# Where seven modulation tiles of the second layer are computed: four among the q, k and v groups, three in the attention steps, and the second q tile's weights awaited by pieces

## What is computed

```python
mod = (s_lat @ ada_w[layer] + ada_b[layer])[:, None, :]     # s_lat = silu(c); mod_c the same with silu(c_ctx)
sh1, sc1, g1, sh2, sc2, g2 = jnp.split(mod, N_MOD, axis=-1) # six parts of 1024
h = modulate(x, norm1_g[layer], sh1, sc1)                   # rms_norm(x, g) * (1 + scale) + shift
h_c = modulate(ctx, norm1_g[layer], csh1, csc1)
q, k, v = qkv_heads(h, odd_w_qkv[i], odd_q_g[i], odd_k_g[i])  # q and k: rms_norm per head of 64
q_c, k_c, v_c = qkv_heads(h_c, odd_w_qkv[i], odd_q_g[i], odd_k_g[i])
y = _merge(neighbourhood_attention(q, k, v, k_c, v_c, odd_rpb[i])) @ odd_w_o[i]
x = x + g1 * y
x = x + g2 * conv_ffn(modulate(x, norm2_g[layer], sh2, sc2), ...)
```

## Time and profile before

| | |
|---|---|
| median of 3 runs | 2199.19 us (2197.61 to 2202.82) |
| the profiled execution, its own time | 2198.84 us |
| its span, of which the rows speak | 2197.2 us |
| TensorE busy | 2080.6 us, 95% of the span |
| VectorE, ScalarE, GpSimd busy | 845.2, 585.0, 71.5 us |
| TensorE's granted clock, mean | 0.984 of full speed |

### The profile page before, as it was taken

One profiled execution on the slowest core, in us unless ns is written; L12 is line 12 of the kernel. 1 busy time (PEld: TensorE's weight loads), 2 busy tenths in 40 slices (PEclk: granted clock), 3 DMA queues, 4 the chain that ended last, 5 costly groups with the idle time before them and its releaser, 6 DMA issues.

```text
span 2197.2 us, 27385 instructions
## 1 busy us (share of the span) xinstructions
PE 2080.6 (95%) x11614; PEld 1389.7 (63%) x11614; DVE 845.2 (38%) x1566; ACT 585.0 (27%) x1002; POOL 71.5 (3%) x119
## 2 busy tenths in 40 slices
PE   7999999999999899999998999999999989999997
PEld 5787887878777479999888833433434333434332
DVE  4355533453583767745465521211111111111012
ACT  4223322342332656534365210000000000000001
POOL 0000000000000320000040000000000000000000
PEclk9999999999999999999999999999999999999998
DMA  9543433422421664545524899999999999999996
GB/s 368 200 152 115 153 115 128 155 79 100 171 77 56 222 219 154 180 159 184 191 97 186 325 370 403 428 428 428 427 428 427 428 428 427 427 427 428 427 409 268
DMA packets 164819, 592.88 MB, mean 270 GB/s; under 512 B 9138, under 2 KB 83890, under 8 KB 139348
## 3 DMA queue, kind: packets, MB, share of 16 engines
q1 hardware_dynamic: 163028, 589.68, 68.0%
q10 hardware_dynamic: 1664, 1.39, 0.2%
HBM read 590.00 MB, written 1.05 MB: 269 GB/s over the span
## 4 chain that ended last, share of the span: by engine, by line
PE 78%; DMA 14%; DVE 3%; ACT 2%; issue 2%; SPq 1%; ACTq 0%; DVEq 0%
PE ps L1007 23%; PE ps L290 14%; PE ps L292 14%; PE ps L291 14%; DMA ring<-in_w_up_dram 10%; DMA ring<-in_ada_w_dram 3%; PE ps L956 3%; PE ps L975 2%; PE ps L436 2%; DVE wr L1141 2%; ACT big L2126 1%; PE ps L1032 1%; PE ps L655 1%; PE ps L444 0%; SPq L2268 0%
## 5 line engine op out<-in xcount | busy, mean ns | idle before, releaser
L1007 PE MATMUL ps<-ring,big 128*64 128x512 f32 x3008 | 684.9, 607 | 56.2 <-DMA ring<-in_w_up_dram 35.6
L1007 PEld LDWEIGHTS ps<-ring,big 128*64 128x64 f32 x3008 | 245.2, 140 | 465.7 <-issue 456.8
L290 PE MATMUL ps<-h_hi,wr 128*128 128x512 f32 (+1 forms) x960 | 337.1, 351 | 2.3 <-DVE big L1378 1.1
L1141 DVE TENSOR_TENSOR wr<-ring,wr 128x1024 fp32r<-128x1024 f32 (+1 forms) x248 | 286.5, 1211 | 134.6 <-ACT wr L1826 134.5
L291 PE MATMUL ps<-h_lo,wr 128*128 128x512 f32 (+1 forms) x960 | 330.4, 344 | 0.0
L292 PE MATMUL ps<-h_hi,wr 128*128 128x512 f32 (+1 forms) x960 | 330.2, 344 | 0.0
L1826 ACT CAST wr<-ring 128x1024 fp32r<-128x1024 f32 (+1 forms) x248 | 239.3, 1032 | 115.9 <-PE ps L292 93.3
L290 PEld LDWEIGHTS ps<-h_hi,wr 128*128 128x128 f32 x960 | 182.5, 190 | 37.1 <-issue 10.4
L291 PEld LDWEIGHTS ps<-h_lo,wr 128*128 128x128 f32 x960 | 182.6, 190 | 22.0 <-issue 1.4
L292 PEld LDWEIGHTS ps<-h_hi,wr 128*128 128x128 f32 x960 | 182.4, 190 | 21.6
L2126 ACT ACTIVATE big<-ps,s 128x128 f32<-128x128 f32 x64 | 24.0, 456 | 357.7 <-PE ps L956 357.7
(11 more groups left out here) (343 smaller groups left out, 2620.8 us busy)
## 6 DMA issues: line engine op xcount, KB each, us to landing
ring<-in_w_gate_dram SPq DMA_DIRECT2D x62, 2048.0 KB, 22.1
ring<-in_w_up_dram SPq DMA_DIRECT2D x59, 2048.0 KB, 18.3
ring<-in_w_down_dram SPq DMA_DIRECT2D x57, 2048.0 KB, 22.0
ring<-in_ada_w_dram SPq DMA_DIRECT2D x24, 2048.0 KB, 11.4
ring<-in_ffn_w_up_dram SPq DMA_DIRECT2D x44, 1024.0 KB, 7.6
ring<-in_ffn_w_down_dram SPq DMA_DIRECT2D x16, 1408.0 KB, 6.2
ring<-in_w_in_dram SPq DMA_DIRECT2D x9, 2048.0 KB, 7.9
ring<-in_odd_w_qkv_dram SPq DMA_DIRECT2D x6, 2048.0 KB, 7.8
```

What stands on the lines that cost most here:

```text
L290: e.matmul(o, l[0], r[0], start=first, stop=False)
L1007: ins = e.matmul(pts[hf][HALF[z], :], lhs[:, k, HALF[z]], wt, start=k == 0, stop=False, skip_group_check=True)
L1141: e.tensor_tensor(wr[:, x], ring[:, x], h.bitcast(F32), SUB).then_inc(s_wlo, 1)
```

## The change

Tiles 17, 18 and 19 move behind groups 5, 9 and 13 of q and k, tile 20 behind the second v group. Their folds come two groups later. Tiles 21, 22 and 23 stay in the attention, in steps 3, 7 and 11, with the fold one step later as before. ScalarE's copies, VectorE's additions and the loads follow. Apart from that, group 4, the first of the second q tile, waits for its weights piece by piece, and for that it is computed ahead of the sums of squares of groups 0 to 2 (`headsum(0)` to `headsum(2)`), which stood ahead of it.

```diff
--- before.py
+++ after.py
@@ -293,6 +293,9 @@
 
 
     NT = [512, 512, 512, L]
+
+    MOD_QK = {5: 17, 9: 18, 13: 19}
+    MOD_NA = {3: 21, 7: 22, 11: 23}
     hz0 = [sum(KC * (NT[i] // L) for i in range(q)) for q in range(5)]
     dg0 = [sum(NT[i] // P for i in range(q)) for q in range(5)]
     sqacc = [(zb[1] if q == 2 else wk[3][:, 0:512])[:, 0:NT[q]] for q in range(4)]
@@ -660,17 +663,20 @@
         wlast[W_QKV] = filled(("qk", 3))
         for g in range(4, 16):
             t = W_QKV + g // 4
-            if g % 4 == 0:
-                e.wait_ge(s_wlo, cum[t + 1])
             if g == 8:
                 e.wait_ge(s_hlo, hz0[3])
+            rows(("qk", g), L if g < 8 else 512, t, g % 4,
+                 ready=(lambda k: e.wait_ge(s_wlo, cum[t] + k // 2 + 1)) if g % 4 == 0 else None)
             if g == 4:
                 headsum(0)
                 headsum(1)
                 headsum(2)
-            rows(("qk", g), L if g < 8 else 512, t, g % 4)
             headsum(g - 1)
             wlast[t] = filled(("qk", g))
+            if g in MOD_QK:
+                mod_rows(MOD_QK[g])
+            if g - 2 in MOD_QK:
+                mod_fold(MOD_QK[g - 2])
         for i in range(2):
             t = W_QKV + 4 + i
             e.wait_ge(s_wlo, cum[t + 1])
@@ -682,6 +688,10 @@
                 ins.then_inc(fullsem(("vv", i, n)))
                 if i == n == 0:
                     headsum(15)
+                if i == 0 and n == 1:
+                    mod_rows(20)
+                if i == 0 and n == 3:
+                    mod_fold(20)
             wlast[t] = filled(("vv", i, 3))
 
 
@@ -729,8 +739,8 @@
             if due is not None:
                 mod_fold(due)
                 due = None
-            if step % 2 and step < 14:
-                due = 17 + step // 2
+            if step in MOD_NA:
+                due = MOD_NA[step]
                 mod_rows(due)
         for c in (6, 7):
             held.discard(full["O", c][0])
@@ -1376,7 +1386,10 @@
             if g == 0:
                 e.wait_ge(*gq_at)
             e.scalar_tensor_tensor(dst, bank(("qk", g))[:, 0:n], gain, r, MULT, MULT).then_inc(freesem(("qk", g)), 1)
+            if g - 1 in MOD_QK:
+                mod_add(MOD_QK[g - 1])
         lo(W_QKV + 5)
+        mod_add(20)
         for g in range(4):
             r = slice(NE * g, NE * g + NE)
             e.tensor_copy(sel[r, :], ident[r, NE * g:NE * g + NE]).then_inc(s_sel4, 1)
@@ -1417,8 +1430,7 @@
             if due is not None:
                 mod_add(due)
                 due = None
-            if step % 2 and step < 14:
-                due = 17 + step // 2
+            due = MOD_NA.get(step)
             if step in (2, 4, 6, 8):
                 lo(W_O, step // 2 - 1, step // 2)
         for i in range(2):
@@ -1987,6 +1999,8 @@
             head_square(g)
             if g:
                 head_root(g - 1)
+            if g - 1 in MOD_QK:
+                mod_copy(MOD_QK[g - 1])
         for i in range(2):
             if i == 0:
                 hi(W_QKV + 5)
@@ -1995,6 +2009,8 @@
                 e.copy(vv[:, n, 512 * i:512 * i + 512], bank(("vv", i, n))[:, :]).then_inc(freesem(("vv", i, n)), 1)
                 if i == n == 0:
                     head_root(15)
+                if i == 0 and n == 2:
+                    mod_copy(20)
 
 
         for step in range(20):
@@ -2013,8 +2029,8 @@
                         e.wait_ge(*rows_used("na", u - 8))
                     e.wait_ge(*filled(("T", u)))
                     e.copy(turned_[u % 8], bank(("T", u))[:, :]).then_inc(freesem(("T", u)), 1)
-            if step % 2 and step < 14:
-                mod_copy(17 + step // 2)
+            if step in MOD_NA:
+                mod_copy(MOD_NA[step])
             if step in (2, 4, 6, 8):
                 hi(W_O, step // 2 - 1, step // 2)
         for m in (22, 23):
@@ -2303,8 +2319,10 @@
         mod(17)
         for i in range(6):
             w(W_QKV + i + 3)
-        for m in range(18, 24):
-            mod(m)
+            if i < 4:
+                mod(18 + i)
+        mod(22)
+        mod(23)
         w(W_O + 1)
         w(W_O + 2)
         e.wait_ge(*filled(("mod", 23)))
```

## The result

| | before | changed |
|---|---|---|
| median | 2199.36 us (6 runs, 2197.61 to 2202.82) | 2208.22 us (6 runs, 2204.55 to 2210.61) |
| profiled execution, its span | 2198.84, 2197.2 us | 2207.77, 2206.1 us |
| GpSimd busy | 71.5 us | 73.9 us |
| mean granted clock | 0.984 | 0.983 |

The ratio is 1.0035, with an interval of [1.0025, 1.0044]: slower by more than 0.2%. The forecast of 2202.5 us would have been no change by that bound, and the measured time lies 1.2 us above the predicted range of 2196.5 to 2207.

A forecast was written before the change was run, and what follows sets the result against it. TensorE was taken as the bound, with VectorE bounding part of the second q tile. 7.1 + 1.65 + 9.6 - 14.7 = +3.65 us on 2198.84 gave 2202.5 us, range 2196.5 to 2207.

The forecast's parts named there:

- The held bank: Second q tile: group 6 waits for group 4's bank until VectorE leaves it, starting at 616.4 not 609.32: +7.1 us.
- Rival C: Query/key stage: group 6 isn't held, the pieces gain 2.7 and 1.65 us; -7.65 us, 2191.2 us; chance 0.11.
- The clock behind it: TensorE after the stall before group 6: the idle time lowers its clock, +1.65 us.
- Work moved in: Behind group 6 TensorE is the bound, so three modulation tiles and four folds come on top: +9.6 us.
- The attention: Attention stage: 66.0 us against 80.7, with modulation tiles moved out and their load waits gone: -14.7 us.
- the first wait: Attention's start: TensorE waits 2.4 us for the first transposes, the tile that filled the rest being gone.
- the clock behind that wait: Attention: the wait for the first transposes lowers TensorE's clock, 1.65 us more.
- VectorE's term: Attention: VectorE's pairs make transposes late, above all in steps 6, 8 and 10: 3.3 us.
- rival A: Attention steps 2 to 9: VectorE's pairs hold TensorE fully, with a second low clock; +6.6, 2205.4 us; chance 0.27.
- Rival B: Attention: VectorE hidden, waits of steps 6 to 10 vanish, clock stays high; -1.3, 2197.5 us; chance 0.14.
- Rival D: Modulation tiles' loads are late all the same, sharing one slot; some 3 us more, 2205.5 us; chance 0.05.
- The step that failed: After the attention: a shift at 792 us reaches the end whole, with no difference arising later: 0 us.

The follow-up runs named there:

- the repeated one: The changed kernel measured again without edits: 2207.3 us, ratio 1.0025 to the kernel before.
- the experiment on the bank alone: Changed kernel with the banks of sums 0 to 2 taken ahead of group 4's, matmuls still by pieces: 2199.35 us, ratio 0.9994.
- the profile with GpSimd's work put off: Changed kernel with GpSimd building the table products only after VectorE has converted the first up tile: 2203.78 us, ratio 1.0015.
- the whole tile: Changed kernel with the second q tile awaited whole again and the old bank order: 2199.69 us, ratio 0.9996.
- the two experiments on the table: Changed kernel with the distance table's loads ahead of the second output and first up tiles', 2204.96 us; or with GpSimd's table work later, 2203.78 us.
- the kernel with the pieces alone: Kernel before with only the second q tile awaited by pieces, all modulation tiles in the attention: 2206.37 us, ratio 1.0022.

## Why the prediction was right and wrong

**The held bank: right, to a tenth.** Group 6 was to start at 616.4 and starts at 618.01, which is 616.5 without the 1.5 us by which this profile is late. The stall is the 4.8 us predicted in this profile (3.67 in the repeated one, where tile 17 ends later), and the experiment on the bank alone removes it. VectorE's first reciprocal starts 6.6 us behind its first conversion where it was 6.2, the 0.4 us predicted. Rival C, which had group 6 free, was mispriced too: with the banks kept, the stretch to the scores is 130.25 - 117.60 = 12.65 us longer than before, where C has 11.4 - 4.35 = 7.05. Its gain of 4.35 us from the pieces does not show.

**The clock behind it: nearly right.** Predicted 1.65, measured 4.28 - 2.97 = 1.3 us. It varies: in the profile with GpSimd's work put off it was low for longer, and the stretch to the scores is 137.13 us instead of 135.68.

**Work moved in: right.** What is left of the stretch is 135.68 - 117.60 - 7.1 - 1.3 = 9.7 us against 9.6. With the whole tile the stretch is 11.3 us longer than before: tile 17's 1.86 us then lie in no stall, and four tiles cost the 11.4 us that rival C gave them.

**The attention: the sum right, two terms not.** 66.17 against 66.0 us; the 2.4 us of the first wait measured 2.70. But the 1.65 us for the clock behind that wait isn't there: with a low clock behind it (scores at 738.16, 2.08 us) the attention takes 66.17, 66.19, 66.06 and 65.91 us in four profiles with this step table, at full clock 65.84, 65.85 and 65.81 in three. It costs 0.4 us at most, since VectorE holds the pairs and TensorE's delay is absorbed. And VectorE's term, which I took as 3.3, is 65.84 - 58.6 - 2.72 = 4.5. Rows of idle time behind the first one make 3.5 us of it in the repeated profile; the other 1.0 us stands in no such row, and where it comes from stays open. That the sum agrees to 0.2 us is luck: the two errors cancel. The transposes are late in steps 6, 8 and 10, as I had said, and VectorE's weight pieces follow each other in 8.5 us, my 8.6 for a pair. But together these three waits are 2.1 us and not over 4, and a second low clock did not come, so rival A's condition isn't met. Rival B falls: the waits did not vanish, and the first division of a pair still takes 0.97 to 0.98 us wherever GpSimd has bias tiles left to build. Rival D falls too, as no load is late.

**The step that failed** is in the first paragraph: "I let a shift at 792 us reach the end whole", and at the end "a difference that arises after it, which I have ruled out by assumption alone". That term was put at nothing, without a row for it. The sum to the attention's end was +3.65 predicted and +3.5 measured; then 3.9 us more arise by 830 us. The chain has these links. The loads of the last output tile and of the first up tile wait for GpSimd's bias units 30 and 32, that is for steps near the end of the attention, and the table's loads stand behind them. The steps behind that point had lost waits, a modulation tile and a fold, so that the attention's end moved towards these loads: from the output tile's load to the attention's end it is 20.4 us before and 15.8 now. GpSimd gets the table 5.3 us later against the attention: 2.3 us because the table's first load stands that much closer to the attention's end, 3.0 because GpSimd starts 15.9 us behind that load where it was 12.9, with the output and up tiles' loads just ahead of it. It works over both conversions, and the last square comes later. Of the 3.9 us, 0.9 lie before the last sum of squares (24.85 to 25.75 us from the attention's end) and some 3 behind it, at low clock. In the repeated profile they are 1.55 and 1.7.

How firm the links are differs. That the overlap lengthens the conversions and the wait is shown by the two experiments on the table, and that it comes from the shortened attention fits the kernel with the pieces alone, where it is absent. That the low clock, the larger part of the cost, belongs to the overlap is shown less well: it came in all four profiles with a wait of over 2.4 us there, but with the banks kept both conversions were long, the clock stayed up and only 0.4 us was lost, and in two kernels without the overlap the clock fell all the same (30.43 and 30.52 us to the feed-forward).

The prediction counted the loads that move, those of the modulation tiles and the ones that they pass; the table's isn't one of them. It is the work around it that moved. That the trace of before already showed the conversion at 796.30 taking 5.54 us and its twin at 806.86 taking 4.64, with GpSimd's row ending between them, was the warning: an overlap that ended in time by 2 us.

**In numbers:** with the missing term the forecast would have been 2202.5 + 3.9 = 2206.4 us; the two measurements are 2207.3 and 2208.22. The term is read from the result, so this adds up the account and tests nothing. What is still missing, 0.9 and 1.8 us, is no more than the 1.8 to 2.0 us by which the execution that the forecast started from lies under the later medians of the kernel before.

## What to carry to other kernels

When a change shortens a stage, list what is issued from inside that stage for the next one: such work keeps its own trigger, and its distance to the next stage shrinks even where nothing of it was edited. When buffers are handed out in program order, changing the order of two takers changes who waits for whom; here that alone cost 5.4 us, and the pieces for which it was done brought nothing. And where another engine bounds a stretch, waits and a low clock on the first one need not be worth their length: in the attention a low clock priced at 1.65 us cost 0.4 at most.

## What the runs showed of the hardware

VectorE's conversion of four pieces, an instruction with two inputs in SBUF, takes 4.63 us alone and 5.1 to 5.55 us where GpSimd multiplies the table over all or a part of it; GpSimd's 12 products take 10.7 us when they are put off behind the conversions, 11.8 to 11.9 when they end as the attention does, and 12.8 to 15.2 over the conversions. Each delays the other. The Trainium skill, "SBUF — State Buffer", section "Who interferes with whom", says that a VectorE instruction with two SBUF inputs contends with a GpSimd instruction that reads SBUF; these rows agree. I had used the page for the bias tiles in the attention, where the divisions did not change (0.97 us), and not here.

The low clock does not follow from a wait's length alone. Before the last sum of squares waits of 2.45, 3.11, 2.65 and 2.63 us were all followed by a low clock; of eight waits between 1.11 and 1.96 us two were (1.12 us both), and six were not, of 1.96 us too. At the first transposes a wait of 2.70 to 2.72 us was followed by it in some profiles of the same code and not in others. What decides between them stays open; no run was made for it.
